# 2nd layer's bias rows added in the fourth expert, GpSimd's split of tile 0 in one piece, first gather evicted ahead of the gate tables

## What is computed

```
logits = xt @ w_router + b_router
top_val, top_idx = top_k(logits, 4);  gates = softmax(top_val)
for each expert e, for the tokens xb that chose it:
    h    = xb @ w1[e] + b1[e]                  # 1024 -> 2048
    act  = min(h_glu, 7) * sigmoid(1.702 * min(h_glu, 7)) * (clip(h_lin, -7, 7) + 1)
    y   += gate * (act @ w2[e] + b2[e])        # 1024 -> 1024
h = h + y;  out = rms_norm(h)
```

## Time and profile before

| | us |
|---|---|
| median of three executions | 1090.05 (1089.8 to 1090.42) |
| profiled execution, its own time | 1088.94 |
| its span | 1087.0 |
| TensorE busy | 986.6 (91%) |
| VectorE busy | 228.6 (21%) |
| ScalarE busy | 117.3 (11%) |
| GpSimd busy | 16.0 (1%) |
| mean granted TensorE clock | 0.985 of 2.4 GHz |
| moved by DMA | 421.31 MB, mean 388 GB/s |

### The profile page before, as it was taken

The page is one execution under the profiler, slowest core; times in us unless marked ns, Lnnn a source line. Parts: engine busy times, 40 slices in busy tenths (PEclk is TensorE's granted clock), DMA queues, the critical chain, the costliest instruction groups (busy, mean ns, idle before and its releaser), DMA issues.

```text
span 1087.0 us, 13893 instructions
## 1 busy us (share of the span) xinstructions
PE 986.6 (91%) x5873; PEld 424.6 (39%) x5873; DVE 228.6 (21%) x526; ACT 117.3 (11%) x231; POOL 16.0 (1%) x19
## 2 busy tenths in 40 slices
PE   7997989999999999988888988898988888898885
PEld 4644543344444444433333333333333333333332
DVE  1576352111111111111111101111111111110013
ACT  1054130000000000000000000000000000000002
POOL 0010010000000000000000000000000000000000
PEclk9998988999999999999999999999999999999998
DMA  9934837999999999999999999999999999999994
GB/s 332 285 127 184 317 147 317 429 405 396 409 426 428 427 427 429 427 430 427 427 429 427 431 427 429 427 428 430 428 429 427 428 429 428 429 427 428 429 428 164
DMA packets 33237, 421.31 MB, mean 388 GB/s; under 512 B 4896, under 2 KB 5408, under 8 KB 7520
## 3 DMA queue, kind: packets, MB, share of 16 engines
q1 hardware_dynamic: 33216, 421.02, 92.7%
HBM read 419.95 MB, written 1.05 MB: 387 GB/s over the span
## 4 chain that ended last, share of the span: by engine, by line
PE 49%; DMA 42%; DVE 5%; ACT 2%; issue 1%; POOL 0%; SPq 0%; POOLq 0%
DMA ring<-in_w_dram 41%; PE bank L1423 21%; PE bank L1459 13%; PE bank L1081 4%; PE bank L1389 3%; PE bank L1382 2%; PE bank L1295 1%; PE bank L1441 1%; ACT work L582 1%; PE bank L1287 1%; ACT work L513 1%; PE bank L1316 1%; DMA h<-in_x_dram 0%; PE bank L1168 0%; PE bank L1351 0%
## 5 line engine op out<-in xcount | busy, mean ns | idle before, releaser
L1423 PE MATMUL bank<-ring,work 128*64 128x512 f32 x2016 | 460.2, 600 | 52.0 <-DMA ring<-in_w_dram 50.0
L1423 PEld LDWEIGHTS bank<-ring,work 128*64 128x64 f32 x2016 | 166.9, 137 | 325.6 <-issue 211.6
L1459 PE MATMUL bank<-ring,work 128*64 128x512 f32 x1024 | 228.5, 599 | 15.5 <-ACT work L582 15.5
L997 DVE TENSOR_SCALAR work<-bank 128x512 f32<-128x512 f32 x32 | 22.1, 692 | 725.8 <-PE bank L1423 725.8
L1459 PEld LDWEIGHTS bank<-ring,work 128*64 128x64 f32 x1024 | 71.7, 138 | 151.7 <-issue 134.1
L579 ACT ACTIVATE work<-work 128x512 f32<-128x512 f32 x32 | 20.2, 632 | 534.7 <-DVE work L997 534.7
L1389 PE MATMUL bank<-work 64*128 64x512 f32 x256 | 63.6, 616 | 0.7 <-ACT work L590 0.7
L1382 PE MATMUL bank<-work,tok 128*128 128x64 bf16 x1024 | 48.2, 194 | 0.0
L1382 PE MATMUL bank<-work 128*128 128x64 bf16 x512 | 46.7, 194 | 0.0
L1382 PEld LDWEIGHTS bank<-work,tok 128*128 128x128 bf16 x1024 | 45.1, 98 | 0.0
L590 ACT ACTIVATE work<-bank 128x512 f32<-128x512 f32 x32 | 19.1, 597 | 223.4 <-PE bank L1459 223.4
(11 more groups left out here) (196 smaller groups left out, 488.2 us busy)
## 6 DMA issues: line engine op xcount, KB each, us to landing
ring<-in_w_dram SPq DMA_DIRECT2D x190, 2048.0 KB, 33.1
ring<-in_w_in_dram SPq DMA_DIRECT2D x8, 1168.0 KB, 17.2
work<-in_w_dram SPq DMA_DIRECT2D x2, 2048.0 KB, 12.0
ring<-in_w_out_dram SPq DMA_DIRECT2D x2, 1024.0 KB, 13.7
ring<-in_w_out_dram SPq DMA_DIRECT2D x1, 2048.0 KB, 20.0
h<-in_x_dram SPq DMA_DIRECT2D x2, 512.0 KB, 4.1
out_dram<-tok SPq DMA_DIRECT2D x4, 256.0 KB, 2.7
tok<-in_b_dram SPq DMA_DIRECT2D x3, 256.0 KB, 16.0
```

The source lines that it names most:

```text
L997: nc.vector.tensor_scalar(glu, bank[2][:, :], LIMIT, None, ALU.min).then_inc(S.glu_ready, 1)
L1423: last = mm(bank[(2, 5)[g]][j * CAP:(j + 1) * CAP, :], xg[:, k * CAP:(k + 1) * CAP], chunk[:, r, g * FF + j * FG:g * FF + (j + 1) * FG], s ...
L1459: last = mm(bank[6][j * CAP:(j + 1) * CAP, :], hidT[:, r, s * CAP:(s + 1) * CAP], chunk[:, r, j * 512:(j + 1) * 512], start=s == 0 and r == 0,
```

## The change

Three edits, in GpSimd's, VectorE's and TensorE's programs.

```
@@ -422,8 +422,8 @@
                 if t == 0:
                     pool.wait_ge(S.left_t0, 1)
                     pool.tensor_copy(parts[0][1], left[:, 0, :]).then_inc(S.part1_t0, 1)
-            pool.wait_ge(S.part1_t0, 1)
-            pool.tensor_tensor(parts[0][2], left[:, 0, :], parts[0][1], ALU.subtract).then_inc(S.part2_t0, 1)
+                    pool.wait_ge(S.part1_t0, 1)
+                    pool.tensor_tensor(parts[0][2], left[:, 0, :], parts[0][1], ALU.subtract).then_inc(S.part2_t0, 1)
...
@@ -1008,10 +1008,10 @@
             left_over(1)
             last_part(0)
             last_part(1)
-            tables()
             dve.wait_ge(S.half_gathered, 1)
             half_out(0, 3)
             half_out(1, 6)
+            tables()
             later_rounds()
...
@@ -1341,15 +1341,14 @@
                     last = nc.tensor.transpose(bank[7][:, t * P:(t + 1) * P], gate_t[:, t, 0:P], ident)
                 last.then_inc(S.gateT_ps, 1)
 
-            def start_row(i):
+            def add_row(i):
 
                 t, nb = divmod(i, 2)
                 if i == 0:
                     pe.wait_ge(S.gateT_sb, 1)
-                    pe.wait_ge(S.extra_done, 1)
                     pe.wait_ge(S.b2_in, 16)
                 mm(bank[Y[i]][:, :], gateT[B_ROWS:P, t * P:(t + 1) * P], b2_sb[:, nb * 512:(nb + 1) * 512],
-                   start=True, stop=False, skip_group_check=True)
+                   start=False, stop=False, skip_group_check=True)
 
             def rows_of(t, i, k):
 
@@ -1383,11 +1382,11 @@
                                       start=i == 0 and t == 0, stop=i == PARTS - 1 and t == TILES - 1)
                 last.then_inc(S.gathered, 1)
 
-            def combine(i, stop=False):
+            def combine(i, start=False, stop=False):
 
                 t, j = divmod(i, 2)
                 last = mm(bank[Y[i]][:, :], gatedT[j * CAP:(j + 1) * CAP, t, :], res[j * CAP:(j + 1) * CAP, :],
-                          start=False, stop=stop, skip_group_check=True)
+                          start=start, stop=stop, skip_group_check=True)
                 if j == 1:
                     last.then_inc(S.combined, 1)
 
@@ -1404,7 +1403,7 @@
                 pe.wait_ge(slot_in[slot_of(c)], (it * LOADS_PER_BODY + ((c - EARLY) // SLOTS + 1)) * 16)
                 return slot(slot_of(c))
 
-            def expert(n, q, it, first=False, second=False):
+            def expert(n, q, it, first=False, second=False, rows=False):
 
 
                 if first:
@@ -1427,13 +1426,15 @@
 
                     if first and c == 0:
                         turn_gates()
-                    if second:
-                        start_row(c)
+                    if rows:
+                        add_row(c)
                 gather(n + 1)
                 if not first:
                     pe.wait_ge(S.res_ready, n)
+                    if second:
+                        pe.wait_ge(S.extra_done, 1)
                     for i in range(4):
-                        combine(i)
+                        combine(i, start=second)
 
                 pe.wait_ge(S.hid_ready, n + 1)
                 apart = lin.rearrange("p (m r) -> p m r", r=W2_ROWS)
@@ -1463,7 +1464,7 @@
 
             first_gather()
             for q in range(UNROLL):
-                expert(q, q, 0, first=q == 0, second=q == 1)
+                expert(q, q, 0, first=q == 0, second=q == 1, rows=q == UNROLL - 1)
             bodies = EXPERTS // UNROLL
             pe.wait_ge(S.extra_done, 1)
             rounds = pe.value_load(extra[0:1, 0:1], min_val=0, max_val=ROUNDS - 1)
```

## The result

| | before | after |
|---|---|---|
| median of five executions, us | 1090.05 (1089.72 to 1091.79) | 1084.87 (1083.7 to 1086.23) |
| ratio, 95% interval | | 0.9947 (0.9927 to 0.9966) |
| profiled execution: its time, span, us | 1088.94, 1087.0 | 1086.23, 1084.4 |
| mean granted clock | 0.985 | 0.988 |

The two profiles differ by 2.6 us only, because the mixer ahead of the change took 2.6 us longer in the one of after (line 904 starts at 151.22 us instead of 148.64 us). So it is chance that the profiles differ by the very 2.6 us of the forecast, and that the 31st load is issued at 268.76 us where 268.7 us was forecast: a gain twice as large was hidden by the longer mixer. Times are therefore counted from line 904's start.

The account below looks back on a forecast made before the run. The weight stream was taken as the bound, its end tied to TensorE's use of the 23rd chunk. -1.45 - 0.68 - 0.5 + 0 = -2.6 us gave 1087.4 us, range 1085.6 to 1089.4.

Parts of the forecast that it names:

- What sets the end: Weight stream: the end is when TensorE has used the 23rd chunk, which releases the 31st load, plus a constant.
- Rival (c): Weight stream: closing the hole at 218 us is a real gain, -3.4 us in all, 1086.6 us; chance 0.10.
- (b): VectorE's stall only moves or is line 893's own, leaving the tables' 0.68 us: 1089.4 us; chance 0.08.
- (d): Bias rows paid in full as TensorE waits for weights: +2.7 us, 1092.7 us; chance 0.03.
- (a): TensorE's clock rises no earlier and takes back 1.05 us: -1.1 us in all, 1089.0 us; chance 0.19.
- Bias rows 0 us: TensorE: second expert 4.8 us shorter, fourth 4.8 us longer before the moment that counts, sum 0.
- GpSimd's part, -1.45 us: Routing: earlier subtraction frees VectorE's line 893 of a 1.77 us stall, net -1.45 us (bounds -1.77 and 0).
- the +0.3 us: Routing: tile 1's variance tensor_scalar on VectorE would be held under the earlier subtraction, at worst +0.3 us.
- Tables, -0.68 us: First gather evicted ahead of the gate tables: TensorE's idle time before the first weight matmul goes, -0.68 us.
- I take -0.5 us: TensorE's clock around the first expert: less time at half clock, -0.5 us, bounds +1.05 and -2.7.
- the far ends of the clock: Extremes of the clock term, bounds +1.05 and -2.7 us, left out of the range.
- The profile's step from the median: Whole kernel: profiled execution 1.1 us below the median before; the same step was taken for the forecast.

Follow-up runs that it names:

- rows_only: Kernel before with only the bias rows moved from the second expert to the fourth: 1090.5 us, ratio 1.0004.
- rows_late: Changed kernel with the four bias rows behind the fourth expert's last W2 chunk instead of its W1 chunks: 1084.63 us, ratio 0.995.
- warm_late: warm_after with the four bias rows behind the fourth expert's last W2 chunk: 1082.84 us, ratio 0.9936.
- rows_split: Changed kernel with two bias rows behind each W2 chunk of the fourth expert: 1083.6 us, ratio 0.9946.
- warm_after: Changed kernel with 19 spare bf16 matmuls in TensorE's idle times, results unused: 1083.96 us, ratio 0.9956.
- pool_only: Kernel before with only GpSimd's subtraction of tile 0 moved ahead of tile 1's 1/rms: 1091.17 us, ratio 1.0; repeated, 1089.79 us, ratio 0.9989.
- tables_only: Kernel before with only VectorE's eviction of the first gather moved ahead of the gate tables: 1086.5 us, ratio 0.9964.
- front_two: Kernel before with the GpSimd and VectorE edits, bias rows left as before: 1085.23 us, ratio 0.9954.
- warm_split: rows_split with 15 spare matmuls, none behind the first tile's ranks or the first gather: 1082.22 us, ratio 0.993.

## Why the prediction was wrong

- **What sets the end: right.** C is 80.08 us and D 815.4 to 815.7 us in all profiles of before and after; the end moved with the 31st load. In every profile of this document the span ends 18.5 to 18.6 us behind the landing of the last weight load. Rival (c) fell with rows_only, (b) with line 893's 0.18 us, (d) with the unchanged C, and (a) had the clock's sign wrong. Where C was shortened by 4.8 us (rows_late, warm_late, rows_split), D rose by 2.6 to 4.4 us (warm_late against warm_after), so the constant holds only as long as the hole ahead of that load is there. The prediction did not say so; the expectation of rows_late did.
- **Bias rows 0 us: right**, 1.0004 (0.9991 to 1.0017).
- **GpSimd's part, -1.45 us: near 1.60 us by two errors that cancel in part.** A shrank by 1.60 us in pool_only. The stall was worth 1.6 us and not 1.77: before, the next instruction (line 888) started 1.86 us behind line 893, 0.09 us ahead of its end, and after the change 0.25 us behind its start. And the +0.3 us was not paid: the tensor_scalar took 0.15 us under the earlier subtraction. The rule of the Trainium skill in "SBUF — State Buffer", section "Who interferes with whom", fits the tensor_scalars of 32 and 4 columns (1.95 and 1.21 us, ended with GpSimd) and the evictions from PSUM, which ran under the subtraction in 0.69 us; the one-column form was not held here. The rule names tensor_scalar for its two-port mode only, and the prediction took that mode for granted with one column. The line behind 893, before:

```profile
155.92 0.24 DVE L888 SCALAR_TENSOR_TENSOR work<-bank,stat,work 128x32 f32<-128x32 f32 x1
```

- **Tables, -0.68 us: right** (0.75 us in tables_only). Together 2.34 us against 2.13.
- **The step that failed: "I take -0.5 us" for the clock.** It was -2.8 us in the profile and -2.7 us in the means of three profiles each. The mechanism and the bound (-2.7) were right, the term was mis-sized. With that bound the sum is -4.8 us, 1085.2 us, close to the 1084.87 us measured; but the range left out "the far ends of the clock", and so the outcome. The gap of 0.68 us was read as one that favours a gain without asking what the whole chain of gaps does: TensorE's waits in the routing fell from 1.2, 0.7 and 0.7 us (lines 1331, 1335 and 1423) to 0, 0.4 and 0 (0.5 us came new, for the last split of tile 1 at line 1368). The clock fell later and rose sooner: half clock for 3.4 us instead of 10.2 (6.7 us in front_two). And the second low stretch, which I kept as an open end, was missing in all seven profiles without the gap, and there in four of the six with it. Which of the gaps makes the clock fall ahead of the routing is not separated; that the last one decides when it rises is what tables_only and the thirteen values of B point to.
- The profile's step from the median (1.1 us) was not the same on both sides: the profiled execution of the kernel before was 1.1 us faster than its median, that of the changed kernel 1.4 us slower. The mixer ahead of the change varies by some us between executions, so one profile is not placed against a median by a constant.

## What to carry to other kernels

An idle gap of TensorE directly ahead of dense matmuls can cost its length and the clock as well (here 0.75 us and 2.3 us); price both, and compare kernels with the gaps filled by spare matmuls to tell the two apart. In a kernel that ends with a saturated stream, find the load at which the queue last ran dry: here, work moved about ahead of it was worth nothing (rows_only), and work moved behind it at most the hole (warm_late, rows_split). When parts are compared, count from a point behind the stretch that scatters.

## What was not expected of the hardware

- In rows_late the clock fell to half at 268 us, though TensorE had been without idle time since 257.84 us. In warm_late the same matmuls stood there in the same order from the second expert's head on, and it did not fall. A TensorE that is always busy can lose its clock; what decides it is open.
- In rows_split the 31st load came 4.8 us sooner and D rose by 2.6 us. The landings of the loads account for it. In the changed kernel the 31st load lands 9.34 us behind the 30th, where 4.90 us is usual, so the hole is 4.4 us long, not 3.1 as the shares of the DMA engines in 6 us stretches had it. rows_split closes it (4.90 us), but its 32nd and 33rd load land 5.8 us behind the one before, which takes back 1.8 us, and its 48th another 0.4 us. That leaves the 2.2 us of the profile.
- One late landing near the 48th load, which never comes back, is in pool_only (1.4 us), warm_late (the 47th, 1.4 us) and warm_split (1.1 us), and in none of the three profiles of the kernel before. Its cause is open. It is of the size of the effects compared here, so a difference of 1 us in D is looked up in the landings before it is explained.
